# Adding drained products of the down pass to the output rows by accumulating transfers instead of GpSimd additions, on one Trainium2 core

## The reference

```python
    h = h + mixed @ w_out[l]
    u = rms_norm(h, norm_mlp_g[l])
    h = h + jnp.square(jax.nn.relu(u @ w_mlp_up[l])) @ w_mlp_down[l]
return rms_norm(h, norm_final_g)
```

## Time and profile before

| | us |
|---|---|
| median of 3 runs (2504.76 to 2504.91) | 2504.76 |
| the profiled execution, its own time | 2504.6 |
| span of its trace | 2502.8 |
| PE busy in the span | 2487.6 (99%) |
| VectorE busy | 2039.5 (81%) |
| ScalarE busy | 1306.0 (52%) |
| GpSimd busy | 621.0 (25%) |

### The profile page before, as it was taken

The page is one execution under the profiler, slowest core; times in us unless marked ns, Lnnn a source line. Parts: engine busy times, 40 slices in busy tenths (PEclk is TensorE's granted clock), DMA queues, the critical chain, the costliest instruction groups (busy, mean ns, idle before and its releaser), DMA issues.

```text
span 2502.8 us, 33406 instructions
## 1 busy us (share of the span) xinstructions
PE 2487.6 (99%) x12100; PEld 2109.9 (84%) x12100; DVE 2039.5 (81%) x2028; ACT 1306.0 (52%) x1622; POOL 621.0 (25%) x455
## 2 busy tenths in 40 slices
PE   9999999999999999999999999999999999999998
PEld 8888888888888888888888888888888888888886
DVE  5868875556479978843599999999999999999997
ACT  6432484344354454433376666666665445544545
POOL 3650131002100000000022233222330554433434
PEclk9999999999999999999999999999999999999999
DMA  6472223222754864454356665666658695545652
GB/s 201 152 269 87 100 89 100 81 74 98 293 194 155 319 245 192 137 161 140 118 171 202 210 194 189 205 208 210 194 190 327 235 310 202 226 160 193 235 219 84
DMA packets 257197, 460.87 MB, mean 184 GB/s; under 512 B 10416, under 2 KB 150288, under 8 KB 243792
## 3 DMA queue, kind: packets, MB, share of 16 engines
q1 hardware_dynamic: 243920, 414.87, 47.6%
q0 software_dynamic: 12928, 44.57, 6.0%
q10 hardware_dynamic: 256, 0.18, 0.0%
HBM read 366.13 MB, written 93.32 MB: 184 GB/s over the span
## 4 chain that ended last, share of the span: by engine, by line
PE 93%; DVE 4%; issue 1%; POOL 1%; ACT 0%; DMA 0%; SPq 0%; DVEq 0%; ACTq 0%; POOLq 0%
PE stream L2388 10%; PE stream L2390 10%; PE stream L2389 10%; PE stream L2779 8%; PE aux L2779 8%; PE aux L2785 4%; PE stream L2785 4%; PE aux L2817 4%; PE aux L2819 4%; PE aux L2818 4%; PE stream L2817 3%; PE stream L2818 3%; PE stream L2819 3%; PE stream L2664 2%; PE stream L2665 2%; PE stream L2666 2%
## 5 line engine op out<-in xcount | busy, mean ns | idle before, releaser
L1599 DVE TENSOR_TENSOR wlo<-raw,whi 128x2048 fp32r<-128x2048 f32 x72 | 172.9, 2402 | 187.3 <-ACT whi L965 187.1
L926 POOL TENSOR_TENSOR hh<-hh,dn_tmp 128x512 f32<-128x512 f32 x112 | 225.9, 2037 | 320.9 <-ACT dn_tmp L1491 320.9
L965 ACT CAST whi<-raw 128x2048 fp32r<-128x2048 f32 x72 | 137.4, 1909 | 231.1 <-PE stream L2390 231.1
L1528 ACT CAST dhi<-d 128x1024 fp32r<-128x1024 f32 x160 | 167.8, 1053 | 167.9 <-PE aux L2819 100.4
L2388 PE MATMUL stream<-uhi,whi 128*128 128x512 f32 (+1 forms) x640 | 243.2, 380 | 0.1
L2389 PE MATMUL stream<-ulo,whi 128*128 128x512 f32 (+1 forms) x640 | 242.3, 379 | 0.0
L2390 PE MATMUL stream<-uhi,wlo 128*128 128x512 f32 (+1 forms) x640 | 242.1, 378 | 0.0
L2321 DVE TENSOR_TENSOR dlo<-d,dhi 128x1024 fp32r<-128x1024 f32 x150 | 216.4, 1460 | 8.0 <-ACT dhi L1528 8.0
L2779 PE MATMUL stream<-sums,uwhi 128*128 128x512 f32 x672 | 185.9, 392 | 0.5 <-ACT states L1401 0.4
L2779 PE MATMUL aux<-sums,uwhi 128*128 128x512 f32 x672 | 185.3, 391 | 0.0
L2817 PE MATMUL stream<-dhi,dsum 128*128 128x512 f32 x448 | 174.4, 389 | 0.6 <-DVE hh L2215 0.6
(11 more groups left out here) (386 smaller groups left out, 6632.9 us busy)
## 6 DMA issues: line engine op xcount, KB each, us to landing
d<-in_w_mlp_down SPq DMA_DIRECT2D x64, 1024.0 KB, 7.3
dsum<-sums_d SPq DMA_DIRECT2D x56, 1024.0 KB, 11.1
raw<-in_w_in SPq DMA_DIRECT2D x48, 1024.0 KB, 5.2
g<-in_w_in SPq DMA_DIRECT2D x32, 1024.0 KB, 7.3
up_b<-in_w_mlp_up SPq DMA_DIRECT2D x32, 1024.0 KB, 8.2
up_a<-in_w_mlp_up SPq DMA_DIRECT2D x32, 1024.0 KB, 5.9
gsum<-usum_d SPq DMA_DIRECT2D x28, 1024.0 KB, 9.6
sums_d<-hlo SPq DMA_DIRECT2D x32, 896.0 KB, 4.2
```

Of the source, the lines that this page charges most:

```text
L926: pool.tensor_tensor(v, v, dn_tmp[r][:], ALU.add).then_inc(s.dn_p, 1)
L1528: nc.scalar.copy(dhi[m % 7][:], parts[j]).then_inc(s.half_hi, 1)
L1599: V.tensor_tensor(wlo[slot][:, 0:width], raw[slot][:, 0:width], whi[slot][:, 0:width].bitcast(F32), ALU.subtract).then_inc(s.lo_ready, 1)
```

## The change

GpSimd no longer adds: for each drain it issues an accumulating transfer from `dn_tmp[r]` to the rows of `hh`, of 128 x 512 float32 or 256 KB, and raises `dn_p` when that transfer has landed. The four semaphores of an earlier use of accumulating transfers (`mix_acc`, each at 16 by then) serve for it under a new name, `acc_dma`. GpSimd's loop over the middle groups is written out, since the waited values now depend on g as a number. Two first states, j = 6 of stage 0 and j = 0 of stage 1, are written by ScalarE (`first_state`, at its places m = 4 and m = 5 of stage 1) and no longer by VectorE (at m = 4 of stage 1).

```diff
@@ GpSimd, dn_adds
                 for r in range(2):
                     pool.wait_ge(s.dn_a, 8 + e + 2 * k + r + 1)
-                    v = hh[:, t + r, dn_cols(n, 1)]
-                    pool.tensor_tensor(v, v, dn_tmp[r][:], ALU.add).then_inc(s.dn_p, 1)
+                    pool.dma_start(hh[:, t + r, dn_cols(n, 1)], dn_tmp[r][:],
+                                   accum_op=ALU.add).then_inc(s.acc_dma[r], 16)
+                for r in range(2):
+                    pool.wait_ge(s.acc_dma[r], 16 * (8 * g + 4 * n + k - 4))
+                    pool.sem_inc(s.dn_p, 1)
@@
-        with pool.Fori(2, GROUPS - 1) as g:
+        for g in range(2, GROUPS - 1):
             dn_adds(g, 0, False, False)
             dn_adds(g, 1, False, False)
@@ ScalarE
+        def first_state(n):
+            j, t = ((6, 2), (0, 0))[n]
+            for r in range(2):
+                nc.scalar.activation(hh[:, t + r, dn_cols(n, 0)], dn_bank(n, j, r)[:], ACT.Copy,
+                                     scale=rs2[:, t + r:t + r + 1]).then_inc(s.dn_v, 1)
+
@@ ScalarE, dn_act
+                if begins and not first and m in (4, 5):
+                    act.wait_ge(s.dn_mm, 7 + 14 + 2 * (m - 4))
+                    first_state(m - 4)
@@ VectorE, dn_dve
-                if begins and m == 4:
-                    dve.wait_ge(s.dn_mm, 7 + 14)
-                    dn_sum(0, 0, 6, 2, True)
-                    dve.wait_ge(s.dn_mm, 7 + 14 + 2)
-                    dn_sum(0, 1, 0, 0, True)
```

More of the change, by code:

```diff
@@ L151, in __init__ @@
         self.row_spl = [nc.alloc_semaphore(f"row_spl{n}") for n in range(2)]
-        self.mix_acc = [nc.alloc_semaphore(f"mix_acc{b}") for b in range(4)]
+        self.acc_dma = [nc.alloc_semaphore(f"acc_dma{b}") for b in range(4)]
         self.mix_t = nc.alloc_semaphore("mix_t")
@@ L870, in _ @@
             pool.wait_ge(s.row_spl[b // 2], 32)
-            pool.dma_start(acc_r[b][:], mixa_d[b], accum_op=ALU.add).then_inc(s.mix_acc[b], 16)
+            pool.dma_start(acc_r[b][:], mixa_d[b], accum_op=ALU.add).then_inc(s.acc_dma[b], 16)
         for i in range(5):
@@ L2671, in turn_mix @@
                 b, w = K_ORDER[p // 4] // 4, p % 4
-                pe.wait_ge(s.mix_acc[b], 16)
+                pe.wait_ge(s.acc_dma[b], 16)
                 if p in (3, 4, 5, 6):
```

## The result

The changed kernel takes **2561.88 us** (median of 5 runs, 2560.17 to 2562.74) against 2504.76 us (5 runs, 2504.31 to 2505.17): ratio 1.0227, 95% interval 1.0215 to 1.0239. It is slower, as forecast, but by 57 us where 14.5 were forecast, far outside the range of 2507 to 2531 us.

The account below looks back on a forecast made before the run. PE was taken as the bound, busy 99%, with only 1.76 us to gain ahead of the down pass's tail. 8.7 + 7.6 - 0.86 - 0.90 = 14.5 us more gave 2519 us, 0.6% slower, range 2507 to 2531 us.

Parts of the forecast that it names:

- So 2.1 us of cover are left, and the cost is nothing: Stage 5, j = 1's second transfer: ScalarE's write ends at 2094.0, PE's j = 4 starts at 2096.08; no cost.
- 7.05 us: Additions as transfers: the second of a pair (r = 1) lands 7.05 us after issue, the first after 5 us.
- The third rival: Odd stages with block sums: j = 4's transfers land late, PE waits 3.9 us in six stages; 2531 us, chance 0.13.
- While ScalarE waits, its casts queue behind that wait, but it is up to seven steps ahead and PE is stopped as well, so nothing further is late: Stage 3, ScalarE's wait behind `add_h(0)`: beyond PE's 8.7 us wait at j = 4, nothing is late.
- The queue behind `add_h`: Stages 3 and 4: additions of j = 1 land behind `add_h`'s 2 MB; PE waits 8.7 and 7.6 us at j = 4.
- Stage 1: First states moved from VectorE to ScalarE: PE's stall in stage 1 goes, a gain of 0.86 us.
- Stage 2: Transfers in place of GpSimd's first two additions, which took 13.49 us: PE's stall in stage 2 goes, gaining 0.90 us.
- the additions do queue: Against the rival that in stages 3 and 4 additions do not queue, landing within 7 us: 2502.8 us, chance 0.10.
- `add_h(0)` did not start earlier: Against the rival that a freed VectorE lets `add_h` start up to 4.98 us earlier: 2509 us, chance 0.12.
- GpSimd issues a pair in 1.74 us: Against the rival that GpSimd cannot issue while VectorE works, PE waiting 9.4 us in 13 stages: 2627 us, chance 0.02.

Follow-up runs that it names:

- experiment 9: The changed kernel with the additions of j = 4 in odd stages given back to GpSimd, all others still transfers: 2520.38 us, ratio 1.0062.
- Experiment 6: The changed kernel with plain copies in place of accumulating transfers, so these sums are left out: 2519.96 us, ratio 1.0064.
- experiment 3: The changed kernel with ScalarE's drain of j = 5 at m = 6 in every stage, before 4 except in stage 2: 2534.05 us, ratio 1.0117.
- experiment 1: The kernel before the change with only the first states moved to ScalarE, additions still on GpSimd: 2503.58 us against 2504.54, ratio 0.9996.

## Why the prediction was wrong

- **The step that failed** is "So 2.1 us of cover are left, and the cost is nothing", which was worked out for one pair, that of j = 1 in stage 5 and PE's wait for it at j = 4, and then used for every pair of all steady stages. At that place it held (stage 5 lost 0.2 us). The cost arose at another pair, that of j = 4 in odd stages, by another path: 58.6 - 18.4 = 40.2 us disappear when j = 4's pairs of the odd stages are GpSimd's again (experiment 9).
- **Two figures of it were wrong together, the landing and the deadline.** The forecast let every pair land 7.05 us after its issue; this pair took from 2208.31 to 2208.9 + 11.9 = 2220.8, 12.5 us. The third rival named the mechanism and allowed 11.1 + 2.05 = 13.2 us, which is enough, but it mis-set the deadline. It let the drain of j = 5 end as late as PE's j = 1, 2 x 2.72 = 5.4 us into the next stage. PE does want `dn_a` only there.
- **What was missed** is what stands behind that drain. On ScalarE these are the casts, behind these VectorE's low parts, and behind these the sum of j = 0, which PE wants at j = 2. In stage 8 it took from 2220.78 + 0.69 = 2221.47 to 2233.12, 11.65 us, from the end of the drain to the end of that sum, and PE stood ready at 2228.06 + 0.23 = 2228.29. So the drain had to end by about 2216.6, 0.8 us ahead of the stage, 6.2 us earlier than I had it. This is an estimate, which takes the chain behind the drain to be as long when it starts earlier. Experiment 6 bears it out: there the drain ended at 2199.18, 0.2 us ahead of stage 8 (2199.37), and PE still waited 0.6 us at j = 2. With the 7.05 us of the forecast the drain would have ended at 2208.31 + 7.05 + 0.69 = 2216.05, just in time. I asked who waits for the transfer, and not what is queued behind the engine that waits. "While ScalarE waits, its casts queue behind that wait, but it is up to seven steps ahead and PE is stopped as well, so nothing further is late" was said of stage 3, and there it held (experiment 9: no other wait of PE); at the drain of j = 5 nothing stops PE meanwhile, and experiment 3 shows the price of the casts behind it: 36.7 us become 3.8.
- **The queue behind `add_h`** was right in mechanism and nearly in size. The pair in stage 3 was to land at 2025.9 and 2027.9; it landed at 2010.4 + 14.8 = 2025.2 and 2011.0 + 16.4 = 2027.4. That this is so near is luck in part: `add_h(0)` began 1.45 us later than in the earlier trace rows, at 2004.54, and its fourth transfer landed after 16.5 us in place of 18.4. The waits forecast were 8.7 and 7.6 us; with nothing else in the way (experiment 9) they are 7.6 and 6.4.
- **The lower clock** is missing from the sum. After those two waits matmuls ran at 1.2 GHz for a while; stages 3 and 4 of experiment 9 lose 18.4 us in all, of which 14.0 are waits in these rows. In stage 8 of the changed kernel it is 7.8 for 4.9.
- **Stage 1** was right: 0.86 us gained. **Stage 2** was wrong. The 0.90 us were to be gained by the transfers; experiment 1 gains them without any, and with the transfers stage 2 lost 1.3 us in place of 0.9. The row of 13.49 us was read as the cost of additions on GpSimd, when VectorE's lateness made it long (4.26 us with VectorE 2.64 us earlier, in experiment 1).
- **The other rivals:** the additions do queue; `add_h(0)` did not start earlier (2004.54 for 2003.09); GpSimd issues a pair in 1.74 us.

## What to carry to other kernels

When an engine that works in order is made to wait for something new, follow its whole queue: the deadline is set by whichever of the later instructions is wanted first, two engines on, and not by the one that waits. A transfer that replaces an engine's work shares its queue and the transfer engines with all other traffic, so time it beside the traffic of its place (here 3.3 us alone, up to 12.6 for the second of a pair beside 8 KB rows), and not by a transfer of the same size elsewhere. Before a slow instruction is replaced, see whether it is slow because of what ran beside it.

## What the runs showed of the hardware

- An accumulating transfer of 256 KB within SBUF, 128 packets of 2 KB, lands after 3.3 us alone (the second of a pair 4.3), a plain one, 64 packets of 4 KB, after 2.3 (2.5); beside 1 MB loads in 8 KB rows 8.6 and 11.9 against 6.3 and 8.0; with those loads in 2 KB rows 6.9 and 8.4.
- A pair of GpSimd additions took 13.49 us while VectorE ran two-input additions without a pause, and 4.26 us where it paused for 0.59 us (experiment 1). The Trainium skill (SBUF — State Buffer, Who interferes with whom) says that a VectorE instruction with two SBUF inputs contends with a GpSimd instruction that reads SBUF; the traces agree, by these two numbers.
- A wait of some 5 us of PE was followed by about 6 us at or near a granted clock of 0.50 (1.2 GHz), and cost 2.9 us more in stage 8.
